# Second mixer of a hybrid encoder layer: GpSimd adds the two halves of each tile's sums, TensorE turns one block in place of two, and VectorE scales it later in its order

## The reference

```python
def dilated_pattern(q, k, v, rel_bias, window, dilation):   # called for (128,1), (512,4), (2048,16)
    ...
    sc = jnp.einsum('brnqhd,brnkhd->brnqhk', qs, ks) * (HEAD_DIM ** -0.5)
    sc = jnp.where(valid, sc + bias, NEG_BIG)
    mx = jnp.max(sc, axis=-1)
    e = jnp.exp(sc - mx[..., None])
    den = jnp.sum(e, axis=-1)
    o = jnp.einsum('brnqhk,brnkhd->brnqhd', e, vs) / den[..., None]
```

## Time and profile before

| what | value |
|---|---|
| time, median of 3 runs | 3468.54 us |
| the profiled execution's own time | 3470.07 us |
| its span, first to last instruction | 3468.3 us |
| second mixer in it | about 1236 to 1649 us, 12% of the span |
| busy over the span: TensorE, VectorE, ScalarE, GpSimd | 96%, 68%, 53%, 54% |
| mean granted TensorE clock | 0.987 |

### The profile page before, as it was taken

The page is one execution under the profiler, slowest core; times in us unless marked ns, Lnnn a source line. Parts: engine busy times, 40 slices in busy tenths (PEclk is TensorE's granted clock), DMA queues, the critical chain, the costliest instruction groups (busy, mean ns, idle before and its releaser), DMA issues.

```text
span 3468.3 us, 54646 instructions
## 1 busy us (share of the span) xinstructions
PE 3341.7 (96%) x17366; PEld 2799.6 (81%) x17366; DVE 2360.2 (68%) x4253; ACT 1853.6 (53%) x3489; POOL 1863.4 (54%) x1365
## 2 busy tenths in 40 slices
PE   8999989999999979999799999999999999999997
PEld 6878878888888868888588888888888888888886
DVE  5556679999898989999455574555655556555554
ACT  3222268888888867777434454343544435443333
POOL 5555534445442257667177750777506776067770
PEclk9999999999999989999899999999999999999998
DMA  5455444444442234343444447444474444744443
GB/s 186 159 181 166 143 133 142 147 161 161 153 153 69 47 86 95 83 105 94 165 128 154 150 159 248 158 152 149 154 267 141 151 154 144 256 160 144 144 136 137
DMA packets 234386, 512.87 MB, mean 148 GB/s; under 512 B 113780, under 2 KB 132668, under 8 KB 214364
## 3 DMA queue, kind: packets, MB, share of 16 engines
q1 hardware_dynamic: 224860, 496.91, 44.4%
q10 hardware_dynamic: 9344, 13.73, 1.1%
HBM read 427.43 MB, written 95.58 MB: 151 GB/s over the span
## 4 chain that ended last, share of the span: by engine, by line
PE 47%; DVE 2%; DMA 1%; ACT 1%; issue 1%; POOL 0%; SPq 0%; DVEq 0%
PE feed_bank L1771 45%; PE feed_bank L1854 1%; PE feed_bank L1762 1%; PE feed_bank L1881 1%; ACT feed_xT L1973 0%; DMA feed_w_split<-scr_wG 0%; DMA feed_comb<-scr_wG 0%; POOL feed_w_split L1727 0%; DMA feed_y_in<-scr_yB 0%; DVE feed_xT L2129 0%; DVE feed_sums L2265 0%; DVE feed_total L2219 0%; ACT feed_w_split L2025 0%; DVE feed_total L2144 0%; DVE feed_ms L2108 0%
## 5 line engine op out<-in xcount | busy, mean ns | idle before, releaser
L1727 POOL TENSOR_TENSOR feed_w_split<-feed_w_raw,feed_w_split 128x1024 fp32r<-128x1024 f32 x352 | 882.0, 2515 | 249.6 <-ACT feed_w_split L2025 236.2
L1771 PE MATMUL feed_bank<-feed_w_split,feed_comb 128*128 128x512 f32 x3552 | 822.1, 391 | 16.6 <-DVE feed_sums L2265 7.8
L1771 PEld LDWEIGHTS feed_bank<-feed_w_split,feed_comb 128*128 128x128 f32 x3552 | 664.6, 188 | 162.5 <-POOL feed_w_split L1727 11.6
L1771 PE MATMUL feed_bank<-feed_xT,feed_w_split 128*128 128x512 f32 x3072 | 701.8, 390 | 2.6 <-DVE feed_xT L2129 2.6
L1771 PEld LDWEIGHTS feed_bank<-feed_xT,feed_w_split 128*128 128x128 f32 x3072 | 578.4, 188 | 123.6 <-DVE feed_xT L2129 3.0
L1052 DVE TENSOR_TENSOR mixa_pT<-mixa_turned,mixa_pT 128x512 fp32r<-128x512 f32 x512 | 350.8, 685 | 62.1 <-ACT mixa_pT L994 52.6
L1724 POOL TENSOR_SCALAR feed_w_split<-feed_w_raw 128x1024 fp32r<-128x1024 f32 x128 | 136.5, 1066 | 464.3 <-PE feed_bank L1771 190.1
L994 ACT ACTIVATE mixa_pT<-mixa_turned 128x512 fp32r<-128x512 f32 x512 | 306.7, 599 | 122.6 <-PE mixa_turned L930 103.1
L875 PE MATMUL mixa_out_acc<-mixa_pT,mixa_v_hl 128*128 128x512 f32 x1028 | 365.1, 437 | 0.7 <-DVE mixa_pT L1052 0.7
L2219 DVE TENSOR_TENSOR feed_total<-feed_total,feed_bank 128x512 f32<-128x512 f32 x352 | 224.4, 681 | 195.8 <-PE feed_bank L1771 192.9
L2040 ACT ACTIVATE feed_rl<-feed_bank 128x512 f32<-128x512 f32 x128 | 76.5, 598 | 524.4 <-PE feed_bank L1771 524.4
(11 more groups left out here) (204 smaller groups left out, 5563.1 us busy)
## 6 DMA issues: line engine op xcount, KB each, us to landing
feed_w_raw<-scr_wT SPq DMA_DIRECT2D x160, 512.0 KB, 3.3
feed_w_split<-scr_wG SPq DMA_DIRECT2D x68, 1024.0 KB, 5.0
feed_w_raw<-w_tail_dram SPq DMA_DIRECT2D x128, 512.0 KB, 3.5
proj_w_raw<-w_in_dram SPq DMA_DIRECT2D x39, 1024.0 KB, 5.3
feed_w_raw<-w_ff_dram SPq DMA_DIRECT2D x64, 512.0 KB, 3.5
scr_table<-scr_bias SPq DMA_DIRECT2D x8, 1520.0 KB, 8.6
proj_x_t<-x_dram SPq DMA_DIRECT2D x20, 512.0 KB, 5.9
mixa_queries<-scr_qA SPq DMA_DIRECT2D x36, 256.0 KB, 4.0
```

The lines of the kernel that those rows point to most:

```text
L1727: pool.tensor_tensor(w_sp[slot][:, 1, :], w_raw[:, slot, :], w_sp[slot][:, 0, :].bitcast(F32), ALU.subtract).then_inc(w_lo, 1)
L1771: mm = pe.matmul(dst, lhs, rhs, start=start, stop=stop)
```

## The change

- GpSimd gets a new step per tile, `halves`: it waits for `sums_out` and adds the two 128 x 128 halves of `oT` into the new `o_sum`. `fold_out` then waits for this (`sum_done`) and transposes one block in place of two. `output` reads and scales 128 x 128 in place of 128 x 256, and `summed` has one addition (L1255's) in place of two.
- On TensorE `fold_out` moves behind `values` of the same pass. On VectorE `output` moves behind `turned_lo`.
- GpSimd's list is dealt out anew: after each tile's `halves` comes one piece of work for the next head: passes 0 to 7 the eight pieces of q and k (k first), 8 to 10 the tables, 11 to 14 the split of v in four pieces (`V_PARTS = 4`) of a quarter each, and a `summed` in every even pass.
- The waits for v being split count four pieces. TensorE's wait for it moves from before `turn` to the head's first `values`. SyncE's order of DMAs stays as it was.

```diff
-        y_part = k.sb("y_part", [P, 2, 2, 2 * P])
+        o_sum = k.sb("o_sum", [P, 2, P])
+        y_part = k.sb("y_part", [P, 2, 2, P])
...
             def load_next(h, nxt):
                 sp.wait_ge(pre_lo, h * PRE + PRE)
                 heads.load_qk(sp, nxt)
-                sp.wait_ge(v_lo, h + 1)
+                sp.wait_ge(v_lo, h * V_PARTS + V_PARTS)
                 heads.load_v(sp, nxt)
...
             def store(h, c):
-                sp.wait_ge(y_ready, h * 16 + (4 * c + 7))
+                sp.wait_ge(y_ready, h * 8 + (2 * c + 4))
...
-            def split_values(h, par):
-                pool.wait_ge(v_dma, h * (16 * V_DMAS) + 16 * V_DMAS)
+            def split_values(h, par, m):
+                if m == 0:
+                    pool.wait_ge(v_dma, h * (16 * V_DMAS) + 16 * V_DMAS)
                 pool.sem_inc(step, 1)
-                pool.tensor_scalar(v_hl[par][:, :, 0:HD], v_in[:], 1.0, 0.0, ALU.mult, ALU.add).then_inc(v_hi, 1)
-                pool.wait_ge(v_hi, h + 1)
-                pool.tensor_tensor(v_hl[par][:, :, HD:2 * HD], v_in[:], v_hl[par][:, :, 0:HD].bitcast(F32), ALU.subtract
-                                   ).then_inc(v_lo, 1)
+                at = slice(m * (VT // V_PARTS), (m + 1) * (VT // V_PARTS))
+                hi, low = v_hl[par][:, at, 0:HD], v_hl[par][:, at, HD:2 * HD]
+                pool.tensor_scalar(hi, v_in[:, at, :], 1.0, 0.0, ALU.mult, ALU.add).then_inc(v_hi, 1)
+                pool.wait_ge(v_hi, h * V_PARTS + m + 1)
+                pool.tensor_tensor(low, v_in[:, at, :], hi.bitcast(F32), ALU.subtract).then_inc(v_lo, 1)
+
+            def halves(N, n):
+
+                pool.wait_ge(o_done, N + 1)
+                pool.sem_inc(step, 1)
+                pool.tensor_tensor(o_sum[:, n % 2, :], oT[:, n % 2, 0:P], oT[:, n % 2, P:2 * P], ALU.add
+                                   ).then_inc(sum_done, 1)
 
             def summed(h, e):
 
-                pool.wait_ge(y_done, h * NU + (2 * e + 4))
-                pool.sem_inc(step, 1)
-                both = y_part[:, e % 2, :, :]
-                pool.tensor_tensor(both[:, :, 0:P], both[:, :, 0:P], both[:, :, P:2 * P], ALU.add).then_inc(y_ready, 1)
-                pool.wait_ge(y_ready, h * 16 + (2 * e + 4))
+                pool.wait_ge(y_done, h * NU + (2 * e + 5))
                 if e % 2 == 0:
                     pool.wait_ge(y_out[e // 2 % 2], h * 32 + (e // 4 * 16 + 16))
                 pool.sem_inc(step, 1)
+                both = y_part[:, e % 2, :, :]
                 pool.tensor_tensor(y_st[:, e // 2 % 2, e % 2 * 2:e % 2 * 2 + 2, :], both[:, :, 0:HD], both[:, :, HD:P],
                                    ALU.add).then_inc(y_ready, 1)
...
                     h = it * 2 + par
-                    summed(h - 1, 7)
-                    for m in range(PRE):
-                        split_pre(h + 1, 1 - par, m)
-                        if m % 2 == 1:
-                            summed(h, m // 2)
-                    split_values(h + 1, 1 - par)
-                    summed(h, 4)
-                    pool.wait_ge(t_dma, h * 32 + 64)
-                    pool.wait_ge(add_done, h * (3 * NU) + 6)
-                    pool.sem_inc(step, 1)
-                    tables(1 - par)
-                    summed(h, 5)
-                    summed(h, 6)
+                    for n in range(NU):
+                        halves(h * NU + n, n)
+                        if n < PRE:
+                            split_pre(h + 1, 1 - par, (n + 4) % PRE)
+                        elif n == PRE:
+                            pool.wait_ge(t_dma, h * 32 + 64)
+                            pool.wait_ge(add_done, h * (3 * NU) + 6)
+                            pool.sem_inc(step, 1)
+                            other_tables(1 - par)
+                            end_tables(1 - par, (0,))
+                        elif n == PRE + 1:
+                            end_tables(1 - par, (1, 2))
+                        elif n == PRE + 2:
+                            end_tables(1 - par, (3,))
+                        elif n < PRE + 3 + V_PARTS:
+                            split_values(h + 1, 1 - par, n - (PRE + 3))
+                        if n == 0:
+                            summed(h - 1, 7)
+                        elif n % 2 == 0:
+                            summed(h, n // 2 - 1)
...
             def fold_out(count, n):
 
-                pe.wait_ge(o_done, count)
-                for part in range(2):
-                    mm = pe.transpose(out_acc[n % 2][:, part * P:(part + 1) * P], oT[:, n % 2, part * P:(part + 1) * P],
-                                      ident[:])
-                mm.then_inc(fold_done, 1)
+                pe.wait_ge(sum_done, count)
+                pe.transpose(out_acc[n % 2][:, 0:P], o_sum[:, n % 2, :], ident[:]).then_inc(fold_done, 1)
...
-            pe.wait_ge(v_lo, 1)
             turn(0, 0)
...
                         turn(N + 1, (n + 1) % NU)
+                        values(N, h, par, n)
                         fold_out(N + 1, n - 1)
-                        values(N, h, par, n)
...
-                        if n % 2 == 1:
-                            ve.wait_ge(y_ready, h * 16 + (n // 2 * 2 + 1))
-                        output(N + 1, (n - 1) % NU)
                         if n % 2 == 0:
                             sums_of_two(N + 1, n + 1)
                         turned_lo(N + 1, n + 1)
+                        if n % 2 == 1:
+                            ve.wait_ge(y_ready, h * 8 + (n // 2 + 1))
+                        output(N + 1, (n - 1) % NU)
```

More of the change, by code:

```diff
@@ L1112, in mixer_b_phase @@
         t_done, hi_done, lo_done, pv_done = (k.sem(n) for n in ("t_done", "hi_done", "lo_done", "pv_done"))
-        o_done, fold_done, y_done = (k.sem(n) for n in ("o_done", "fold_done", "y_done"))
+        o_done, sum_done, fold_done, y_done = (k.sem(n) for n in ("o_done", "sum_done", "fold_done", "y_done"))
         y_ready = k.sem("y_ready")
@@ L1118, in mixer_b_phase @@
         PRE = 8
+        V_PARTS = 4
         FIRST_ORDER = (4, 0, 5, 6, 7, 1, 2, 3)
@@ L1188, in _, with other_tables @@
                 pool.sem_inc(s, 16)
-            pool.memset(oT[:, 1, :], 0.0).then_inc(set_done, 1)
+            pool.memset(o_sum[:, 1, :], 0.0).then_inc(set_done, 1)
             pool.memset(rden[:, SLOTS - 1:SLOTS], 0.0).then_inc(set_done, 1)
             pool.memset(y_part[:, 1, :, :], 0.0).then_inc(set_done, 1)
-            pool.sem_inc(o_done, 1)
-            pool.sem_inc(y_done, 1)
+            pool.sem_inc(sum_done, 1)
+            pool.sem_inc(y_done, 2)
             pool.sem_inc(y_ready, 1)
-            def tables(par):
+            def other_tables(par):
                 near = t_near[:].rearrange("p (v n) -> p v n", v=7)
@@ L1202, in tables, with end_tables @@
                                      ).then_inc(t_done_pool, 1)
+            def end_tables(par, residues):
+                near = t_near[:].rearrange("p (v n) -> p v n", v=7)
                 sided = lambda e, r: t_end[par][:, e, r, PAD:P - PAD].rearrange("p (x s n) -> p x s n", s=2, n=PAD)
-                for r in range(RES):
+                for r in residues:
                     for x, z in ((0, r), (r + 1, RES)):
@@ L1217, in _ @@
             pool.wait_ge(t_dma, 32)
-            tables(0)
+            other_tables(0)
+            end_tables(0, range(RES))
             def split_pre(h, par, m):
-                if m == 0:
+                if m == 4:
                     pool.wait_ge(qk_dma, h * (16 * QK_DMAS) + 16 * QK_DMAS)
@@ L1228, in split_pre @@
                 pool.tensor_scalar(hi, raw, 1.0, 0.0, ALU.mult, ALU.add).then_inc(pre_hi, 1)
-                pool.wait_ge(pre_hi, h * PRE + m + 1)
+                pool.wait_ge(pre_hi, h * PRE + (m - 4) % PRE + 1)
                 if m < 4:
@@ L1232, in split_pre @@
                     pool.tensor_tensor(low, raw[HD:P, :], low.bitcast(F32), ALU.subtract).then_inc(pre_lo, 1)
[L1233 removed]
+                    pool.wait_ge(pre_lo, h * PRE + (m - 4) % PRE + 1)
                 else:
                     pool.tensor_tensor(kT[par][1][:, at], raw, hi.bitcast(F32), ALU.subtract).then_inc(pre_lo, 1)
[L1237 to L1238 removed]
+            def split_values(h, par, m):
+                if m == 0:
+                    pool.wait_ge(v_dma, h * (16 * V_DMAS) + 16 * V_DMAS)
                 pool.sem_inc(step, 1)
[L1240 to L1251 removed]
+                at = slice(m * (VT // V_PARTS), (m + 1) * (VT // V_PARTS))
[8 more added lines that the diff above has]
+                                   ).then_inc(sum_done, 1)
+            def summed(h, e):
+                pool.wait_ge(y_done, h * NU + (2 * e + 5))
                 if e % 2 == 0:
@@ L1320, in values @@
                 pe.wait_ge(lo_done, N * 2 + 2)
-                pe.wait_ge(y_done, N + 1)
+                pe.wait_ge(y_done, N + 2)
+                if n == 0:
+                    pe.wait_ge(v_lo, h * V_PARTS + V_PARTS)
                 for c, vt in enumerate(tiles, c0):
```

(11 more changed lines are left out.)

## The result

The changed kernel takes 3482.78 us, the median of six runs from 3479.99 to 3484.52, against 3468.97 us of the kernel before on the same chip: a ratio of 1.0036 with a 95% interval from 1.0025 to 1.0046, 14 us slower. In a second comparison it was 1.0031 (1.0018 to 1.0043). The profiled execution's span is 3481.4 us in place of 3468.3, 13.1 us more, and the whole of it lies in the second mixer: from its first tile's bias to its last one's are 419.9 us in place of 406.7.

A forecast was written before the change was run, and what follows sets the result against it. A four-engine ring of 6.14 us per two tiles was taken as the bound, VectorE just behind TensorE. From 3468.5 us, -6 + 21 + 6 + 1.6 - 0.5 = +22 gave 3490.5 us; range 3465 to 3512 us.

The forecast's parts named there:

- late store: Heads 1 to 7: SyncE's third store, queued behind v's load, keeps GpSimd and then TensorE waiting; 21 us lost.
- steady tiles: Second mixer's ordinary tiles: one transpose less per tile shortens them; 6 us gained, bounds 0 and 16.6.
- clock: Granted clock drops after four new standstills of 3.8 us, 1.5 us each; 6 us lost, bounds 0 and 12.
- start: Mixer's first tiles: 2.4 us gained by an earlier first turn, TensorE's fold waits 4.0 us; net 1.6 us lost.
- end: Mixer's end: the last addition of 0.74 us goes and `halves` comes in; 0.5 us or so gained.
- the ring: Chain of bias, exp, turn, fold, values and scores through four engines, 6.14 us per two tiles; loses 0.055 us a tile.
- `halves` in the way of the fold: GpSimd's new 0.46 us addition before TensorE's fold costs nothing if GpSimd comes to it in time.
- 1.1 us of cover: Time from the GpSimd sum being ready, 1404.4 to 1404.5, to the fold's new place behind values, about 1405.54.
- GpSimd's own spare: 0.1 us GpSimd has over in its list, added to the fold's 1.1 us before TensorE stands still.
- hold of v's first small DMA: SyncE's queue: time v's first small transfer is held back; 2.6 us taken, between 0.4 and 5.1.
- Behind a jump: Three heads where the 1.86 us jump back gives the store more time: 3.1 us late, 1.9 us lost each.
- The rival in which GpSimd is the bound in every tile: GpSimd's additions a tenth slower add 6 us on top of the forecast, 3496 us; chance 0.04.

The follow-up runs named there:

- two single cuts: Kernel before, half of the tiles' sums left out: VectorE scaling 128 of 256 columns, 3470.01 us; or TensorE doing one transpose per tile, 3465.35 us.
- both mends: Changed kernel with the third store moved ahead of v's load in SyncE's order and a separate semaphore for k's load: 3463.18 us, 0.9979 of before.
- first mend: Changed kernel with a head's third store moved ahead of v's load in SyncE's order: 3469.28 us, 0.9994 of before.
- both cuts: Kernel before with one transpose per tile and 128 columns scaled, half of the tiles' sums left out: 3464.76 us, 0.9984 of before.

## Why the prediction was right, step by step

The forecast was 3490.5 us, 22 us slower, and the kernel is 14 us slower, inside the range of 3465 to 3512 and by the mechanism named. The sum is 9 us above the 13.1 us that the profile's span grew. The late store alone was put 12 us too high, and smaller errors the other way take 3 us of that back, so the total looks better than its largest term:

| term, us | forecast | in the profile |
|---|---|---|
| steady tiles | -6 | -3.8 |
| late third store | +21 | +9.3 |
| clock | +6 | +1.3 at a standstill, +3.3 at the jumps |
| start | +1.6 | +3.1 |
| end | -0.5 | -0.1 (what is left of the 13.1) |

What each step came to:

- **The steady tile.** I took 6 us of gain from the ring, with 0 and 16.6 us as bounds, and said that VectorE's 0.13 us a tile would not count. It is 3.8 us, 0.03 us a tile. The two single cuts show it: 0.01 us a head from VectorE, 0.46 from TensorE. The ring should have given 0.055 us a tile, but nearly all the gain lies in one tile of four; what holds the other three no run separated. So the ring of 6.14 us, read off two tiles, is not the limit in every tile.
- **`halves` in the way of the fold.** It takes the 0.46 us forecast and is hidden in the steady tile, with 1.1 us of cover; v in one piece used the cover up and left the 2.8 us computed from it. The 0.1 us of GpSimd's own spare that was added to it fits too: in the three late heads without a clock drop the loss is 1.3 us less than GpSimd's wait.
- **The late store.** The place, the chain and the pattern were right for four heads. The sum was too large in one term, the hold of v's first small DMA. I took 2.6 us between 0.4 and 5.1. The middle of two bounds was a guess and not a reading. In the changed kernel that issue takes 1.05 to 1.40 us (1.14 in the row below), and from v's first DMA to the store are 12.9 to 13.4 us (14.4 in the first, where another of the small issues took 1.41 us as well), where I had 14.85. So the store was 3.0 to 3.6 us late, once 4.7, and not 5.0; the loss per head 1.7 to 2.3 us, once 4.6, and not 3.8. With 1.1 us in place of 2.6 the prediction's own sum gives 4 x 2.3 + 3 x 0.4 = 10.4 us in place of 21.

```profile
1404.24 0.40 SPq L94 DMA_DIRECT2D mixb_v_in<-scr_vB  x1
1404.83 1.14 SPq L102 DMA_DIRECT2D mixb_v_in<-scr_vB  x1
```

- **Behind a jump** I had 1.9 us of loss for three heads. There GpSimd doesn't wait at all: the store of 1365.56 us lands 2.0 us later, and `summed` comes at 1367.84. The smaller hold takes 1.5 us off the 3.1, and the slowed tile behind the jump gives the store still more time. The kernel with k's semaphore has the same late store and one jump without a clock drop, the second, and there GpSimd does wait:

```profile
1463.79 0.46 POOL L1273 TENSOR_TENSOR mixb_y_st<-mixb_y_part 128x128 f32<-128x128 f32 x1 [1.41 <-DMA scr_yB<-mixb_y_st]
```

  This is the 1.6 us that are left of 3.1, and nearly all of it is covered: that head takes 50.55 us, and 50.43 in the kernel with both mends. The term of 21 us was 10.6 us, of which about 1.3 us are the slowed clock of the first such head (its loss is 4.6 us at a wait of 4.69, where the others lose 1.3 us less than they wait).
- **The clock.** I counted four drops behind the new standstills, 6 us. One came there, at 1317 us. But a drop came behind each of the three jumps, where the kernel before had one:

```profile
1354.62 0.69 DVE L1459 CUSTOM_DVE_ANT_0 mixb_prob<-mixb_score,mixb_t_own 128x512 f32<-128x512 f32 x1 [2.20 <-issue]
...
1355.00:1360.00 5.00, 2.70 (x13) 2.40 (x12) 4.61 (x19) 2.50 (x5) 2.00 (x3) 0.76 0.27 49
1457.00:1462.00 5.00, 2.83 (x16) 2.43 (x14) 4.38 (x18) 2.14 (x5) 1.33 (x3) 0.80 0.49 100
1560.00:1565.00 5.00, 2.67 (x13) 2.30 (x12) 4.61 (x19) 2.40 (x5) 1.90 (x3) 0.74 0.30 55
```

  These are VectorE's row at the first jump and the stretches behind the three of them, whose granted clock (the third value from the right) is 0.74 to 0.80. With the jump's own wait of 2.20 us in place of 1.86 that is 3.3 us. With the 1.3 us of the standstill the sum is 4.6 us and near the 6 forecast, but this is luck: three of the four standstills brought no drop, and the jumps, where most of it lies, were not in the forecast.
- **The start** was forecast at 1.6 us lost, with a wait of 4.0 us for the fold: it is 3.1 us lost, the wait 3.64 us, and the tile behind it ran at half clock, which I hadn't counted. The 2.4 us from the earlier first turn did come: from the second tile's bias to the third's are 6.57 us in place of 8.96.

The rival in which GpSimd is the bound in every tile falls with the first mend: in the kernel with both mends, at 48.47 us a head, GpSimd waits for ScalarE's copy before 97 of the sums, 94.1 us in all. The Trainium skill, GPSIMD Engine Reference, section Engine selection, prefers VectorE for such additions and calls GpSimd about 2x slower with two inputs. The trace agrees: the subtraction that splits v, 128x2048 from two inputs in SBUF, took 2.29 us on VectorE at the mixer's start in the kernel before and 4.60 us on GpSimd. No run has the new addition itself on VectorE. But where the slower engine has room and the sum has 1.1 us of cover its 458 ns cost nothing.

## What to carry to other kernels

When an engine that had only work for later gets a step on the path, look through everything that it may stand behind in its list: each semaphore it waits for, and the queue that feeds this semaphore. Here the new step and its cover were right, and the loss came from a store that a moved split had pushed behind 25 DMA issues, from one semaphore that covered two loads, and for some 3 us from clock drops behind the jumps, whose cause is open; one line moved in the queue's order and one more semaphore turned 14 us of loss into 7 us of gain. And if two engines look equally full, cut each alone: here VectorE, busy 98% of the time, got 0.13 us a tile back and nothing came of it.

## What was unexpected of the hardware

- How long SyncE is held at v's first small DMA goes with what was issued before it: 8.41 us at the changed kernel's start, right behind the loads of k and q; 5.10 us with the load of q 4 us old (4.95 to 6.43 us in the seven heads of the kernel before); 1.05 to 1.40 us where those loads have landed. No run varied this alone. The small ones behind it follow one another by 0.41 to 0.56 us, all but a few.
- The jump back costs a granted clock drop in some cases and not in others, with much the same gap. In the three profiles with the late store (the changed kernel twice, and the one with k's semaphore) 8 of 9 jumps have one; in the kernel before and the ones with one or both cuts 2 of 12; in the ones with the store moved and with both mends 2 of 6; with the fold moved back, alone or with the scaling, 4 of 6; with v in one piece 3 of 3; with the scaling alone moved back 1 of 3. So a late store isn't needed for it. Nor does the length of the gap decide: VectorE's gap is 1.86 us at the kernel before's first jump, with a drop, and 2.46 us at the second jump of the kernel with the scaling moved back, without one. A drop costs 1.5 us in the tile it hits. What decides is open; no run varied it alone.
